# Feed-forward operands at start addresses 16 bytes apart modulo 256

## What is computed

```python
def swiglu(x, wg, wu, wd):
    return (jax.nn.silu(x @ wg) * (x @ wu)) @ wd

for l in range(DEPTH):                       # DEPTH = 2
    x = x + 0.5 * swiglu(rmsnorm(x, ffn1_norm[l]), ffn1_wg[l], ffn1_wu[l], ffn1_wd[l])
    h = rmsnorm(x, mix_norm[l])
    x = x + (even_mixer(h, ...) if l % 2 == 0 else odd_mixer(h, ...))
    x = x + 0.5 * swiglu(rmsnorm(x, ffn2_norm[l]), ffn2_wg[l], ffn2_wu[l], ffn2_wd[l])
return rmsnorm(x, final_norm)                # D_MODEL 1024, D_FF 2816, SEQ 512
```

## Time and profile before

| what | value |
|---|---|
| median of three runs | 1916.97 us |
| lowest and highest run | 1916.32 and 1918.15 us |
| span of the profiled execution, first to last instruction | 1912.0 us |
| what lies around the span, against the median | 5.0 us |
| TensorE matmul busy | 1878.0 us, 98% |
| TensorE weight load busy | 1640.7 us, 86% |
| VectorE busy | 1305.9 us, 68% |
| ScalarE busy | 920.3 us, 48% |
| granted TensorE clock | 9 tenths or more of full speed in every slice |

### The profile page before, as it was taken

One profiled execution on the slowest core, in us unless ns is written; L12 is line 12 of the kernel. 1 busy time (PEld: TensorE's weight loads), 2 busy tenths in 40 slices (PEclk: granted clock), 3 DMA queues, 4 the chain that ended last, 5 costly groups with the idle time before them and its releaser, 6 DMA issues.

```text
span 1912.0 us, 31629 instructions
## 1 busy us (share of the span) xinstructions
PE 1878.0 (98%) x11410; PEld 1640.7 (86%) x11410; DVE 1305.9 (68%) x1921; ACT 920.3 (48%) x1589; POOL 222.7 (12%) x205
## 2 busy tenths in 40 slices
PE   8999999999999999999999999999999999999998
PEld 6899988778888889997888999888776788999887
DVE  7899843567656679983357989435796677999434
ACT  5455532427556445552243555333487543555323
POOL 0100000210233210000021000001146221000001
PEclk9999999999999999999999999999999999999999
DMA  5233332222211323333222232322321022333331
GB/s 179 69 109 110 112 107 99 92 89 55 91 45 47 104 71 111 102 117 111 88 88 89 89 121 98 132 88 88 103 86 45 23 69 86 111 110 108 112 105 60
DMA packets 36718, 177.72 MB, mean 93 GB/s; under 512 B 12560, under 2 KB 14096, under 8 KB 16160
## 3 DMA queue, kind: packets, MB, share of 16 engines
q1 hardware_dynamic: 34496, 173.24, 26.8%
q10 hardware_dynamic: 1952, 2.85, 0.5%
q0 software_dynamic: 192, 0.59, 0.1%
HBM read 174.56 MB, written 2.10 MB: 92 GB/s over the span
## 4 chain that ended last, share of the span: by engine, by line
PE 90%; DVE 4%; ACT 3%; issue 1%; DMA 1%; POOL 0%; ACTq 0%; POOLq 0%; DVEq 0%
PE ps L359 29%; PE ps L361 28%; PE ps L360 28%; PE ps L1690 1%; DVE wl L287 1%; ACT wh L283 1%; PE ps L1713 1%; PE ps L1222 1%; PE ps L1294 1%; DMA raw<-in_units 1%; DVE u L2503 0%; PE ps L1421 0%; PE ps L1284 0%; PE ps L1204 0%; DVE xgl L412 0%
## 5 line engine op out<-in xcount | busy, mean ns | idle before, releaser
L359 PE MATMUL ps<-xgh,wh 128*128 128x256 f32 (+1 forms) x1472 | 495.7, 337 | 9.7 <-DVE xgl L708 3.9
L361 PE MATMUL ps<-xgh,wl 128*128 128x256 f32 (+1 forms) x1472 | 490.9, 334 | 0.0
L360 PE MATMUL ps<-xgl,wh 128*128 128x256 f32 (+1 forms) x1472 | 489.9, 333 | 0.0
L287 DVE TENSOR_TENSOR wl<-raw,wh 128x2048 fp32r<-128x2048 f32 (+1 forms) x92 | 212.7, 2312 | 351.6 <-ACT wh L283 351.4
L359 PE MATMUL ps<-tmh,wh 128*128 128x256 f32 (+1 forms) x1344 | 411.0, 306 | 0.0
L360 PE MATMUL ps<-tml,wh 128*128 128x256 f32 (+1 forms) x1344 | 410.1, 305 | 0.0
L361 PE MATMUL ps<-tmh,wl 128*128 128x256 f32 (+1 forms) x1344 | 409.6, 305 | 0.0
L283 ACT ACTIVATE wh<-raw 128x2048 fp32r<-128x2048 f32 (+1 forms) x92 | 174.6, 1898 | 358.1 <-PE ps L361 356.9
L359 PEld LDWEIGHTS ps<-xgh,wh 128*128 128x128 f32 x1472 | 278.0, 189 | 42.6 <-issue 5.3
L360 PEld LDWEIGHTS ps<-xgl,wh 128*128 128x128 f32 x1472 | 278.1, 189 | 29.5 <-issue 2.2
L361 PEld LDWEIGHTS ps<-xgh,wl 128*128 128x128 f32 x1472 | 278.1, 189 | 27.8
(11 more groups left out here) (318 smaller groups left out, 2654.1 us busy)
## 6 DMA issues: line engine op xcount, KB each, us to landing
raw<-in_units SPq DMA_DIRECT2D x160, 1024.0 KB, 5.0
out<-xg SPq DMA_DIRECT2D x4, 512.0 KB, 2.6
relb<-in_rpb SPq DMA_DIRECT2D x64, 24.0 KB, 2.2
x<-in_xT ACTq DMA_DIRECT2D x2, 512.0 KB, 6.9
x<-in_xT SPq DMA_DIRECT2D x2, 512.0 KB, 7.6
raw<-in_units SPq DMA_DIRECT2D x2, 256.0 KB, 5.6
raw<-in_units ACTq DMA_DIRECT2D x2, 256.0 KB, 9.5
xg<-in_last_gain ACTq DMA_DIRECT2D x1, 512.0 KB, 3.7
```

The source lines that it names most:

```text
L287: nc.vector.tensor_tensor(wl[:, c % 2, 0:n], raw[:, c % 2, 0:n], wh[:, c % 2, 0:n].bitcast(F32), ALU.subtract).then_inc(w_lo, 1)
L359: nc.tensor.matmul(dst, lh, rh, start=first, stop=False, skip_group_check=onto)
L360: nc.tensor.matmul(dst, lh, rl, start=False, stop=False, skip_group_check=onto)
L361: return nc.tensor.matmul(dst, ll, rh, start=False, stop=last, skip_group_check=onto)
```

## The change

It changes start addresses and nothing in the order of the work. Every engine issues the same instructions in the same order with the same waits; only the writes of the quarters (`right_hi`, `right_lo`) have another shape, 1024 elements in a row for four rows of 256.

- A pad `phase` of 16 floats (64 bytes) moves the whole shared region from place 192 to place 0.
- The four sums get strides of 1088 floats and an offset of 4 floats (16 bytes) times 4f + t. Sum t of feed-forward f stands at place 16 (4f + t): sixteen places, each used by one sum of one feed-forward.
- The down stage's tiles (`a_part`, tile k2 = 0 or 1 of a unit) stand at place 32 (2f + k2) for an even unit and 16 bytes further for an odd one: again sixteen places.
- The three quarters in `xgh`/`xgl` begin 16 floats into the buffer, at place 64, each in one piece of 1024 floats (before: rows of 256 columns, 2048 bytes apart, at place 0). In the up stage the same buffers are used as before, at place 0.
- In the mixers the pads `bT_phase`, `mxl_phase` and the larger `xcp_end` keep `bTh`/`bTl` at place 192 and `qrh`, `cqh`, `dTh` at place 0; `mxh`, `mxl`, `uh`, `ul`, `knh`, `knl`, `vbh`, `vbl` move from place 192 to place 0. `vbh`/`vbl`, moving operands against `bTh`/`bTl`, thereby begin 64 bytes behind them modulo 256, where they began at the same place.

```diff
+        sb("phase", [P, 16])
...
-        tmh = sb("tmh", [P, 4, 4, HALF], F32R, ffn_mem)
-        tml = sb("tml", [P, 4, 4, HALF], F32R, ffn_mem)
+        tmh = sb("tmh", [P, 4 * (4 * HALF + 64)], F32R, ffn_mem)
+        tml = sb("tml", [P, 4 * (4 * HALF + 64)], F32R, ffn_mem)
...
-        ash = sb("ash", [P, 2, SEQ], F32R, ffn_mem)
-        asl = sb("asl", [P, 2, SEQ], F32R, ffn_mem)
+        ash = sb("ash", [P, 2 * (SEQ + 64)], F32R, ffn_mem)
+        asl = sb("asl", [P, 2 * (SEQ + 64)], F32R, ffn_mem)
...
         pN = sb("pN", [P, 2, 5 * P], F32, even_mem)
+        sb("bT_phase", [P, 48], F32, even_mem)
...
+        sb("mxl_phase", [P, 16], F32, even_mem)
         mxl = sb("mxl", [P, 4, SEQ], F32R, even_mem)
...
-        sb("xcp_end", [P, 12], F32, odd_mem)
+        sb("xcp_end", [P, 60], F32, odd_mem)
...
-        def right(b, k):
+        def sum_tile(buf, f, t):
+
+            o = t * (4 * HALF + 64) + 4 * (4 * f + t)
+            return buf[:, o:o + 4 * HALF].rearrange("p (k n) -> p k n", k=4)
+
+        def right(f, b, k):
 
             if b < B11:
-                return tmh[:, b, k, :], tml[:, b, k, :]
-            rows, cols = {B11: (k, slice(0, HALF)), B21: (4 + k, slice(0, HALF)), B22: (4 + k, slice(HALF, SEQ))}[b]
-            return xgh[:, rows, cols], xgl[:, rows, cols]
+                return sum_tile(tmh, f, b)[:, k, :], sum_tile(tml, f, b)[:, k, :]
+            i = (B11, B21, B22).index(b)
+            return right_tiles(xgh, i)[:, k, :], right_tiles(xgl, i)[:, k, :]
+
+        def right_tiles(buf, i):
+
+            o = 16 + (0, 8, 4)[i] * HALF
+            return buf[:, :, :].rearrange("p k s -> p (k s)")[:, o:o + 4 * HALF].rearrange("p (k n) -> p k n", k=4)
...
-        def a_part(i, k2):
-
-            return (ash[:, k2, :], asl[:, k2, :]) if i % 2 == 0 else (tmh[:, 0, 2 * k2:2 * k2 + 2, :], tml[:, 0, 2 * k2:2 * k2 + 2, :])
+        def a_part(f, i, k2):
+
+            o = k2 * (SEQ + 64) + 8 * (2 * f + k2) + (4 if i % 2 else 0)
+            return tuple(m[:, o:o + SEQ] for m in ((tmh, tml) if i % 2 else (ash, asl)))
```

More of the change, by code:

```diff
@@ L546, in prod_pe @@
             for k in range(4):
-                mm = three(ps[:, bank, 0:HALF], lh[:, k * P:(k + 1) * P], ll[:, k * P:(k + 1) * P], *right(b, k),
+                mm = three(ps[:, bank, 0:HALF], lh[:, k * P:(k + 1) * P], ll[:, k * P:(k + 1) * P], *right(f, b, k),
                            k == 0 and a in (A11, A12, S3, S4), k == 3, a in (S2, S1, A22))
@@ L686, in right_part @@
             rows, cols = ((slice(0, 4), slice(0, HALF)), (slice(4, 8), slice(0, HALF)), (slice(4, 8), slice(HALF, SEQ)))[i]
-            return xgh[:, rows, cols], xgl[:, rows, cols], xn[:, rows, cols]
+            return right_tiles(xgh, i), right_tiles(xgl, i), xn[:, rows, cols]
         def sums_hi(act, f, t):
             act.wait_ge(s_sum, (4 + 8 * RP) * f + (1, 3, 3, 4)[t])
-            nc.scalar.activation(tmh[:, t], tm32[:, t], ACT.Copy).then_inc(s_hi, 1)
+            nc.scalar.activation(sum_tile(tmh, f, t), tm32[:, t], ACT.Copy).then_inc(s_hi, 1)
         def sums_lo(dve, f, t):
             dve.wait_ge(s_hi, (7 + 12 * RP) * f + t + 1)
-            nc.vector.tensor_tensor(tml[:, t], tm32[:, t], tmh[:, t].bitcast(F32), ALU.subtract).then_inc(s_lo, 1)
+            nc.vector.tensor_tensor(sum_tile(tml, f, t), tm32[:, t], sum_tile(tmh, f, t).bitcast(F32), ALU.subtract).then_inc(s_lo, 1)
         def right_hi(act, f, B, i):
@@ L708, in right_lo @@
             nc.vector.tensor_tensor(l, x32, h.bitcast(F32), ALU.subtract).then_inc(s_lo, 1)
-        def a_part(i, k2):
-            return (ash[:, k2, :], asl[:, k2, :]) if i % 2 == 0 else (tmh[:, 0, 2 * k2:2 * k2 + 2, :], tml[:, 0, 2 * k2:2 * k2 + 2, :])
+        def a_part(f, i, k2):
+            o = k2 * (SEQ + 64) + 8 * (2 * f + k2) + (4 if i % 2 else 0)
+            return tuple(m[:, o:o + SEQ] for m in ((tmh, tml) if i % 2 else (ash, asl)))
         def a_tile(i, k2, j=0):
-            a = a32[:, bass.ds(2 * i + 4 * j + k2, 1), :]
-            return a if i % 2 == 0 else a.rearrange("p o (a b) -> p (o a) b", a=2)
+            return a32[:, bass.ds(2 * i + 4 * j + k2, 1), :]
         def a_hi_act(act, f, i, j=0):
@@ L725, in a_hi_act @@
                     act.wait_ge(s_lo, left_count(f, RP - 1, 12))
-                nc.scalar.activation(a_part(i, k2)[0], a_tile(i, k2, j), ACT.Copy).then_inc(a_hi, 1)
+                nc.scalar.activation(a_part(f, i, k2)[0], a_tile(i, k2, j), ACT.Copy).then_inc(a_hi, 1)
         def a_lo_dve(dve, f, i, j=0):
@@ L730, in a_lo_dve @@
                 dve.wait_ge(a_hi, 22 * f + 2 * i + 4 * j + k2 + 1)
-                h, l = a_part(i, k2)
+                h, l = a_part(f, i, k2)
                 nc.vector.tensor_tensor(l, a_tile(i, k2, j), h.bitcast(F32), ALU.subtract).then_inc(a_lo, 1)
@@ L743, in down_pe @@
                     o = k2 * D + b * P
-                    mm = three(ps[:, b, :], wh[:, s, o:o + P], wl[:, s, o:o + P], *a_part(i, k2),
+                    mm = three(ps[:, b, :], wh[:, s, o:o + P], wl[:, s, o:o + P], *a_part(f, i, k2),
                                i == 0 and isinstance(j, int) and k2 == 0, False)
@@ L922, in ffn_pe @@
             if last:
-                final_pe(pe, c + 10, lambda k2: a_part(10, k2))
+                final_pe(pe, c + 10, lambda k2: a_part(f, 10, k2))
             else:
-                down_last_pe(pe, c + 10, lambda k2: a_part(10, k2))
+                down_last_pe(pe, c + 10, lambda k2: a_part(f, 10, k2))
         def ffn_act(act, f, B, n, last):
```

## The result

The changed kernel takes 1920.82 us (median of 16 runs, 1917.65 to 1924.17), beside 1917.35 us for the kernel before in 16 runs (1913.7 to 1918.88). The ratio is 1.0018, 95% interval 1.001 to 1.0025: slower by 3.5 us, between 2 and 5 us, where 10 us less was forecast. That is outside the noise, under the 0.2% that the prediction counted as a change, and within its range; the direction was wrong.

What follows compares the result with a forecast made beforehand. TensorE was taken as the bound: matmul count times pitch, set by start addresses modulo 256 bytes. Quarters -11.5, sums +10.4, down stage -6.9, mixers -2.1 make -10.1 us; span 1901.9 plus 5.0 gives 1906.9 us, range 1883 to 1929.

Steps and rivals of the forecast that it cites:

- The bound: Up, product and down stages: TensorE never idles, so time is the count of matmuls times their pitch.
- The theory: All stages: pitch depends on where the moving operand begins against the stationary one, modulo 256 bytes; 10.1 us less in all.
- the rival that places do nothing: All stages: pitches differ for another reason; 1917.0 us, or 1901.6 if the step between blocks is the cause; chance 0.12.
- Part 1: Product stage, 2304 matmuls on quarters of the input, place 0 to 64: 120.0 to 115 ns, -11.5 us.
- Part 2: Product stage, 3072 matmuls on sums, place 192 to sixteen places: +10.4 us, from -7.6 to +19.3.
- Part 3: Down stage, 2064 matmuls of 512 columns, place 192 to sixteen places: -6.9 us, from -25.0 to +11.1.
- Part 4: Mixers: tiles moved from place 192 to 0 give -1.6 us, `vbh`/`vbl` -0.5; together -2.1 us.
- Part 5: Writes by ScalarE and VectorE to the shifted tiles: taken at nothing, with no new wait of TensorE.
- the check on VectorE's idle time: Product stretch of 130 us: without its 9.2 us idle VectorE needs 120.8 us, so it does not become the bound.
- The bounds: Pitch at unseen places: 110 to 120 ns at 256 columns, 220 to 240 at 512.
- The step from span to median: Whole kernel: 5.0 us added to the forecast span of 1901.9 us, giving 1906.9 us.
- the rival on the other side: Sums' old place was the exception: other places slow at 256 columns, +16.7 us, 1933.7 us; chance 0.23.

Runs made afterwards that it cites:

- experiment 10: Changed kernel with sums and quarters at place 112 and all down-stage tiles at place 0: 1895.7 us, ratio 0.9887 to the kernel before.
- experiment 3: Changed kernel with the quarters laid out as before, rows 2048 bytes apart at place 0: 1928.53 us, ratio 1.005 to the kernel before.
- experiment 8: Changed kernel with quarters at place 0 in one piece, sums at 192, down stage at 0: 1903.94 us, ratio 0.9924 to the kernel before.
- experiment 9: Changed kernel with the first quarter at place 0, other quarters and sums at 192, down stage at 0: 1896.94 us, ratio 0.9895 to the kernel before.
- experiment 1: Changed kernel with the four sums back at place 192 in all feed-forwards: 1922.49 us, ratio 1.0025 to the kernel before.
- experiment 2: Changed kernel with sums and quarters at place 192 and all down-stage tiles at place 0: 1908.17 us, ratio 0.9946 to the kernel before.
- experiments 4 to 7: Four changed kernels, sums, quarters and down-stage tiles of each feed-forward sharing one place, sixteen places in all: 1921.7, 1924.1, 1930.8, 1923.9 us beside 1920.1.

## Why the prediction was wrong

*The bound* was right: the time is a count of matmuls times their pitch, TensorE has no idle time in the three stages, and a change of addresses, with the quarters' rows in one piece, moved the kernel by 3.5 us one way and, in experiment 10, 22 us the other.

*The theory* was half right. Start addresses modulo 256 bytes move the pitch, and the rival that places do nothing is out. The Trainium skill ("SBUF — State Buffer", "Who interferes with whom") says that TensorE never waits on anyone. The conclusion drawn from it, that the change would do nothing, falls with that rival; whether TensorE waits for another engine's access, no run here shows. What failed is the step to "the pitch depends on where the moving operand begins": the rows of before held two places, and the prediction read each place's pitch off one history. Place 192 had 113.3 ns because quarters at place 0 ran before it (experiments 3, 8 and 9). Behind quarters at 64 it has 117.5 to 117.8 ns (experiments 1 and 3), and with all product tiles at 192 it had 113.3 ns until a delay and 117.8 behind it (experiments 2 and 4 to 7).

*Part 1, the quarters*: forecast -11.5 us, measured -4.7. This is the step that was most wrong. The lean to 115 ns for a difference of 64 bytes rested on symmetry with 192 and its 113.3 ns. Place 64 settles at 117.8 and shows 113.3 only behind some sums; over all quarters, with waits, the pitch went from 279.1 / 2304 = 121.1 to 119.1 ns, 2.0 ns less where 5.0 were taken.

*Part 2, the sums*: forecast +10.4, measured +11.1. The reason that they held a good place and would lose by being spread was right. The middle taken for the unseen places was too low: 116.7, where these fourteen average 118.1. The base was too low as well: 113.3 is the pitch of a settled step, and the sums of before took 353.6 / 3072 = 115.1 ns with the steps that switch place, and with waits. The two errors cancel, so that the agreement is luck.

*Part 3, the down stage*: forecast -6.9, measured -3.2. Direction right, size half. The fourteen unseen places were taken at 230 ns; settled they average 232.5.

*Part 4, the mixers*: `knh` came to 226.7 ns as said, for 0.6 us. `mxh`, forecast at 0.6 us, gained nothing that shows; what `uh` and `vbh` gained cannot be told apart from the lower clock in that stage. One reading was wrong: in the matmuls with `bTh` and `dTh` these two are the moving operands, and `vbh` and the tile in `xgh` the stationary ones. For `dTh` this changes nothing, as both stand at place 0; for `bTh` the forecast of 0.5 us would by the prediction's own theory have been 0.6.

*Part 5*: no new wait at the changed kernel's pitch, as said. At 113.3 ns one did appear, and on ScalarE, which the check on VectorE's idle time could not see: it was one copy behind one split, not an engine that is full.

*The bounds*: 110 ns as the fast end was taken from a run of 128-column matmuls, as the price of a weight load. Nothing settled under 113.3 ns, but no run shows that the weight load sets a limit.

*The step from span to median*: I took 5.0 us for what lies around the span. It is 1.8 us (1920.72 us for the profiled execution of the changed kernel, span 1918.9); the other 3.2 us are most likely stretches at the lower clock, which the profiled execution of before happened to be without. This shifts no difference, since the kernel before has them too.

In sum, parts 1 and 3 make 10.5 us by the traces, of 13.9 us between the forecast, 1906.9, and the median. The gains fell short while the loss of part 2 came in full, and that turned the sign.

By its number the rival that places do nothing, 1917.0 us, lies nearest, but by luck: gains and losses of over 3 us cancel. By its mechanism the rival on the other side came nearest for the places that no row had shown: at 256 columns they cost more than the middle, 118.1 ns on average. It had 0.23.

What stays open is the mechanism below the pitch. The runs show that the pitch has a memory, and that a delay or a pass through another place can switch it; they don't show which two streams meet, what decides behind a delay, nor why 112 settles well at 256 columns and 0 at 512. The work of ScalarE and VectorE is an unlikely cause: with all tiles at place 0, 16 or 32 the pitch is from round 1 on the same to 0.1 ns in every step but the last, whatever they do there. No experiment moved `wh` or `wl`.

## What to carry to other kernels

Where TensorE runs back to back, read the pitch from start times, by tile, and not one number per shape: here equal matmuls differ by 6%, and the cause is the moving operands' start addresses, their own and those of the matmuls before. A pitch seen at one address belongs to that address together with what ran before it; before betting on it, run the stage with all tiles at one place, see where it settles, and whether a delay moves it. When the pitch falls, look for single instructions on the other engines that stand ahead of the one that TensorE waits for; moving one copy was worth 7 us in the traces.

## What the runs showed that was not expected

One start address has several settled pitches: 192 at 256 columns had 113.3 and 117.5 to 117.8 ns, 208 had 116.7 and 119.3. In experiment 2 a pause of 0.24 us ended the fast one for the rest of a stage, 7 rounds of 168 matmuls, and moving a tile to a place that is itself slow brought it back. In another execution a pause of nearly the same length left the fast one in place.

Several settled pitches are whole multiples of 6.67 ns: 113.3, 120.0, 226.7 and 233.3 are 17, 18, 34 and 35 of them. Others, such as 117.8, are not.

At 512 columns no settled pitch was under 226.6 ns, at 256 none under 113.3, over sixteen places. The fast end of the prediction's bounds, 110 and 220, was not reached.
